# The feed-forward up-projection's low parts leave GpSimd, its product moves ahead of the next convolution, and the routing's long steps take one operand from PSUM

## The reference, cut to what matters

```python
v1, i1 = lax.top_k(sc[..., 0, :], 16)
v2, i2 = lax.top_k(sc[..., 1, :], 16)
cand = (v1[..., :, None] + v2[..., None, :]).reshape(B, S, 8, 256)
cidx = (i1[..., :, None] * 128 + i2[..., None, :]).reshape(B, S, 8, 256)
best, pos = lax.top_k(cand, 16)
idx = jnp.take_along_axis(cidx, pos, axis=-1)
```

```python
up = hn @ w_up                                   # 1024 -> 2 x 2816
gate = gelu(causal_dwconv(up[..., :2816], conv_f_w, conv_f_b))   # 3 taps along the tokens
return (gate * up[..., 2816:]) @ w_down
```

## Time and profile before

| | us |
|---|---|
| median of 3 runs (lowest, highest) | 1558.96 (1558.39, 1559.15) |
| the profiled execution, its own time | 1558.32 |
| its span in the profile | 1556.3 |
| TensorE busy (PE) | 1465.7 (94%) |
| VectorE busy (DVE) | 1059.1 (68%) |
| ScalarE busy (ACT) | 719.7 (46%) |
| GpSimd busy (POOL) | 326.4 (21%) |
| mean DMA rate | 157 GB/s |

### The profile page before, as it was taken

How to read it: one execution, slowest core, us unless ns; L and a number is a source line. 1 busy time by engine, 2 the same in 40 slices (tenths; PEclk the granted TensorE clock), 3 DMA queues, 4 the chain that set the end, 5 groups by cost and what they waited for, 6 DMA issues and landing times.

```text
span 1556.3 us, 26173 instructions
## 1 busy us (share of the span) xinstructions
PE 1465.7 (94%) x10784; PEld 1323.0 (85%) x10784; DVE 1059.1 (68%) x1702; ACT 719.7 (46%) x1031; POOL 326.4 (21%) x158
## 2 busy tenths in 40 slices
PE   7989989999999999999999999999986889988998
PEld 7989879989999999998887888887974678888876
DVE  5565664886937777788888756555797844577764
ACT  5762554544444344444444455445541544544443
POOL 4000000698980000000000000001252420233310
PEclk9999999999999999999999999999997999999999
DMA  6334455455555555455554575554421343444553
GB/s 230 125 122 136 125 180 192 133 168 181 171 174 171 164 163 162 157 165 165 165 163 163 190 244 191 189 189 150 136 95 54 109 149 109 151 158 152 163 181 116
DMA packets 66933, 245.11 MB, mean 157 GB/s; under 512 B 7424, under 2 KB 7552, under 8 KB 66560
## 3 DMA queue, kind: packets, MB, share of 16 engines
q1 hardware_dynamic: 66816, 243.45, 47.9%
HBM read 242.37 MB, written 1.05 MB: 156 GB/s over the span
## 4 chain that ended last, share of the span: by engine, by line
PE 73%; DVE 13%; ACT 7%; POOL 4%; issue 2%; DMA 0%; DVEq 0%; ACTq 0%; POOLq 0%
PE bank L415 73%; DVE A L1474 4%; DVE A L1467 4%; ACT whi L999 4%; POOL wlo L2236 3%; ACT A L999 2%; DVE A L1471 2%; DVE wlo L1471 1%; PE bank L424 1%; DVE A L1468 1%; ACT L999 1%; DVE A L2013 0%; POOL small L2242 0%; DMA xres<-in_x 0%; DVE hTl L1474 0%
## 5 line engine op out<-in xcount | busy, mean ns | idle before, releaser
L999 ACT ACTIVATE whi<-raw 128x1024 fp32r<-128x1024 f32 x448 | 471.9, 1056 | 423.0 <-PE bank L415 422.0
L1471 DVE TENSOR_TENSOR wlo<-raw,whi 128x1024 fp32r<-128x1024 f32 x333 | 408.1, 1228 | 318.7 <-ACT whi L999 318.3
L415 PE MATMUL bank<-hTh,whi 128*128 128x256 f32 x1944 | 560.5, 288 | 28.0 <-DVE wlo L1471 15.1
L415 PE MATMUL bank<-hTh,wlo 128*128 128x256 f32 x1944 | 550.3, 283 | 0.0
L415 PE MATMUL bank<-hTl,whi 128*128 128x256 f32 x1944 | 549.5, 283 | 0.0
L415 PEld LDWEIGHTS bank<-hTh,whi 128*128 128x128 f32 x1944 | 368.1, 189 | 37.8 <-DVE wlo L1471 19.2
L2236 POOL TENSOR_TENSOR wlo<-raw,whi 128x1024 fp32r<-128x1024 f32 x115 | 298.1, 2601 | 410.0 <-ACT whi L999 406.4
L415 PEld LDWEIGHTS bank<-hTl,whi 128*128 128x128 f32 x1944 | 369.2, 190 | 0.8 <-issue 0.7
L415 PEld LDWEIGHTS bank<-hTh,wlo 128*128 128x128 f32 x1944 | 367.7, 189 | 0.0
L415 PE MATMUL bank<-whi,hTh 128*128 128x512 f32 (+2 forms) x552 | 217.9, 395 | 4.2 <-POOL wlo L2236 2.3
L415 PE MATMUL bank<-wlo,hTh 128*128 128x512 f32 (+2 forms) x552 | 215.0, 390 | 0.0
(11 more groups left out here) (151 smaller groups left out, 1487.4 us busy)
## 6 DMA issues: line engine op xcount, KB each, us to landing
raw<-in_u SPq DMA_DIRECT2D x128, 512.0 KB, 3.3
raw<-in_v SPq DMA_DIRECT2D x128, 512.0 KB, 3.4
raw<-in_w_up SPq DMA_DIRECT2D x44, 512.0 KB, 3.3
raw<-in_w_down SPq DMA_DIRECT2D x22, 512.0 KB, 4.1
raw<-in_w_in_t SPq DMA_DIRECT2D x18, 512.0 KB, 3.7
raw<-in_w_in_g SPq DMA_DIRECT2D x16, 512.0 KB, 3.4
raw<-in_w_out SPq DMA_DIRECT2D x16, 512.0 KB, 3.4
raw<-in_w_pq SPq DMA_DIRECT2D x16, 512.0 KB, 4.3
```

The lines of the kernel that those rows point to most:

```text
L415: return e.matmul(o, l, r, start=st, stop=sp_, skip_group_check=True)
L999: return e.activation(o, i, func, **kw)
L1471: return e.tensor_tensor(o, a, b, op)
```

## The change

It has three parts.

1. `on_pool` no longer gives GpSimd the odd units that are prepared during the up-projection: 22 low parts move to VectorE (units 3 to 43 of `w_up` and unit 1 of `w_down`). Unit 1 of `w_up` stays on GpSimd.
2. In VectorE's `lin_T`, `after(u)` becomes `before(u)`: the product of pair j-1 is issued ahead of the wait for pair j and of its convolution.
3. In the routing, `iota16` and a copy of the second half of the values are put into PSUM bank 7; the one-hot comparison reads `iota16` there and writes to banks 0 to 3 in four pieces of 512; the product reads those banks, in four pieces; the sum for `cand` reads the copy in bank 7.

```diff
 def on_pool(i):
     slot = i - 2
     if BASE["u"] <= slot < BASE["u"] + 62:
         return True
-    if BASE["w_up"] <= slot < BASE["w_up"] + 44:
-        return i % 2 == 1
     if slot == BASE["w_xk"] or i in (1, BASE["w_pq"] + 1, BASE["w_up"] + 1):
         return True
...
-            def lin_T(u0, units, evict=None, after=None, per=1, steps=(1,)):
+            def lin_T(u0, units, evict=None, before=None, per=1, steps=(1,)):
                 for u in range(units):
                     i = u0 + u
                     lo(i + 2)
+                    if before:
+                        before(u)
                     if (u + 1) * per % 2 == 0:
                         q = pair[0]
                         if evict:
                             e.wait_ge(s["w"], i + 1)
                             evict((u + 1) * per - 2, t3(banks[4 + q % 3][:, :], 2))
                         pair[0] += 1
-                    if after:
-                        after(u)
                     side.step(steps[(i + 1) % len(steps)])
...
                 shape = [P, 8, 16, 16]
+                v2p = t3(banks[7][:, 16:16 + P], 8)
+                own(e.tensor_copy(v2p, vv[:, :, 1, :]))
                 again()
                 own(tt(t4(cand, 8, 16), vv[:, :, 0, :].unsqueeze(3).to_broadcast(shape),
-                       vv[:, :, 1, :].unsqueeze(2).to_broadcast(shape), ALU.add))
+                       v2p.unsqueeze(2).to_broadcast(shape), ALU.add))
...
                 for q in range(2):
                     ps = t3(posf[:, q * P:(q + 1) * P], 8)
-                    o4 = t4(oh, 8, 16)
+                    part = [P, 2, 16, 16]
                     again()
-                    own(tt(o4, ps.unsqueeze(3).to_broadcast(shape),
-                           K_("iota16").unsqueeze(1).unsqueeze(1).to_broadcast(shape), ALU.is_equal))
+                    for g in range(4):
+                        own(tt(t4(banks[g][:, :], 2, 16), ps[:, 2 * g:2 * g + 2, :].unsqueeze(3).to_broadcast(part),
+                               banks[7][:, 0:16].unsqueeze(1).unsqueeze(1).to_broadcast(part), ALU.is_equal))
                     again()
-                    own(tt(t4(oh2, 8, 16), o4, iv[:, :, q, :].unsqueeze(2).to_broadcast(shape), ALU.mult))
+                    for g in range(4):
+                        own(tt(t4(oh2[:, g * 512:(g + 1) * 512], 2, 16), t4(banks[g][:, :], 2, 16),
+                               iv[:, 2 * g:2 * g + 2, q, :].unsqueeze(2).to_broadcast(part), ALU.mult))
...
+            own(e.tensor_copy(banks[7][:, 0:16], K_("iota16")))
             own(e.tensor_copy(t3(iota_b[:, :], P), K_("iota").unsqueeze(2).to_broadcast([P, P, 2])))
             lin_T(BASE["w_pq"], 16)
```

More of the change, by code:

```diff
@@ L327, in build @@
         candw = a2(24064, 2048)
-        oh = a2(26112, 2048)
         oh2 = a2(28160, 2048)
```

## The result

| | before | after | ratio (95%) |
|---|---|---|---|
| median, us | 1558.68 (4 runs) | 1533.37 (4 runs) | 0.9838 (0.9808 to 0.9868) |
| lowest to highest | 1557.89 to 1559.15 | 1529.98 to 1536.88 | |
| profiled execution, us | 1558.32 | 1530.26 | |
| its span | 1556.3 | 1528.0 | |

The change is faster by 1.6%. The forecast was 1530.1 us, in a range of 1528.0 to 1540.5. The profiled execution is the one to compare with the forecast's sum (1529.5), since both are one execution; it took 0.8 us more.

What follows compares the result with a forecast made beforehand. It took the up-projection to be bound by a ring of waits and the routing by GpSimd's low parts. 18.8 + 1.1 + 8.9 = 28.8 us off 1558.32 gave 1529.5, forecast as a median of 1530.1, range 1528.0 to 1540.5.

Steps and rivals of the forecast that it cites:

- The hold: Up-projection: GpSimd's low part holds VectorE's tensor_scalar, which opens a convolution, at 2.29 us; without it 0.35.
- The up-projection, 18.8 us: Parts one and two bring 145.55 us down to 126.7, 22 pairs at 5.76 us; bounds 18.8 and 9.4.
- The ring: Up-projection waits before the change: gate copy, convolution, product, R4h, high part, Gelu, next high part, next gate copy; 6.71 us a turn.
- the new ring: Up-projection after the change: convolution, Gelu, high part, low part, product; 4.52 us, 5.0 with hand-overs, against 5.76 allowed.
- w_down, 1.1 us: Third unit of w_down: its 0.91 us wait for a low part goes, 1.1 us with the restart.
- The routing, 8.9 us: TensorE's losses to GpSimd's slowed low parts, 4.8 and 4.1 us in two blocks, are gained; GpSimd at 2.43 us.
- Pieces at 0.68 us: Routing: a VectorE piece of 512 with a PSUM input takes 0.68 us, sixteen of them 10.9 us a block.
- The cover: Routing, second block: VectorE idles 12.58 us for TensorE's pass 30, so the block may grow by 12.6 us without cost.
- The copy into bank 7: Routing: by the skill's rule VectorE's copy of values into PSUM may be held by GpSimd; at most 2.4 us, covered.
- the routing gave its gain: Answers the rival that the routing gives nothing and its 8.9 us stay: 1539.0 us, chance 0.10.
- the stage kept nothing of its loss: Answers the rival that the up-projection keeps half, TensorE waiting some 0.4 us a pair: 1539.5 us, chance 0.10.
- the tensor_scalar went to 0.35 us: Answers the slower rival: the tensor_scalar stays at 2.29 us, held by something other than GpSimd; 1566.4 us, chance 0.03.

Runs made afterwards that it cites:

- the all-SBUF pieces: The kernel after with the routing's pieces of 512 kept but every operand, including the cand sum's, in SBUF: 1550.69 us, routing stretch 464.0 us.
- the kernel with half the steps in PSUM: The kernel after with the one-hot comparison writing to SBUF, so the products read two SBUF inputs in pieces of 512: 1531.59 us, routing stretch 448.3.

## Why the prediction was right, point by point

- *The hold.* "GpSimd's step holds it, and its length is not its own": right, shown twice over by the 0.35 us of the tensor_scalar without GpSimd and by the hold that moves to the tap once the tensor_scalar has a PSUM operand.
- *The up-projection, 18.8 us.* Measured 18.6, at 126.9 us. The reason was half right. The ring and its slow link were as read, and TensorE waits for nothing in the stage now. But the prediction said that parts one and two "must be taken together", and each alone gives all of it: part one with a ring of 5.76 us, just at the bound, part two with 2.53 us of slack in front of the convolution. The way of counting the new ring (4.52 us, 5.0 with hand-overs), whole durations and hand-overs end to end, comes out too long, since an instruction begins before its forerunner's printed end (without the reordering VectorE's low part at 1404.55 lasts 1.22 us, and the next step starts at 1405.68). Here it erred to the safe side; without the reordering it made me expect 134 us or more.
- *w_down, 1.1 us.* Measured 1.2 at the third unit, whose wait is gone, and 1.2 to the end.
- *The routing, 8.9 us.* Measured 9.0; GpSimd at 2.4 us a part and no wait of TensorE for it. Counting by pace and not by the 6.9 us of printed waits was right: the run without part three has 7.0 us of waits and 9.0 us more time. That the cure is the PSUM operand and not the cutting is shown by the all-SBUF pieces.
- *Pieces at 0.68 us.* 0.69, writing to PSUM included, and started every 0.60 us. The cover in the second block was 16.63 us, more than the 12.58 counted on.
- *The copy into bank 7.* The prediction allowed, from the Trainium skill's rule, that it "may be held". It was not: in both blocks it begins 0.01 or 0.02 us behind the start of a low part of GpSimd and takes 0.28 us.
- *Not in the sum.* The head of the kernel, which the change barely touches (one copy of 0.17 us), came out 1.0 us shorter and the stretch of the second layer 1.5 us longer. The head is chance: the kernel with half the steps in PSUM has 226.3 us there again. In the second layer the granted clock is 0.95 and 0.88 from 1070 to 1090 us, where the kernel before has 1.00 over the same work. The two nearly cancel, and that they do is luck.
- *The median.* The sum was good to 0.5 us (28.3 of span against 28.8). The median was 3.3 us above the forecast, since "a microsecond or two either way" was too little. TensorE's half clock in the first layer (last section) costs 6 us where it shows; that it is what lifted the median is likely but not shown, since the two longer runs were not profiled.
- *The rivals.* None came: the routing gave its gain, the stage kept nothing of its loss, the tensor_scalar went to 0.35 us.

## What to carry to other kernels

Where a short VectorE step looks long, set its end against GpSimd's ends: if the two go together, the step is being held, its busy time is not work, and an engine that seems full may have room. Give such a step a PSUM operand or shift it in time, but look which instruction stands next with its tensors in SBUF, since the hold can go there; and don't cut an SBUF step into pieces beside an engine that is always ready to start. A ring of waits costs only what it exceeds the bound by, so of two cures that shorten it one may do; check how much slack that one leaves. Add up a ring from starts, not from printed durations.

## What the runs showed of the hardware that I had not expected

**A cut makes the loser.** Beside back-to-back low parts of GpSimd, an SBUF step of 2048 elements takes 4.36 us and slows GpSimd to 3.40 us a part on average; four steps of 512 take 11.19 us and GpSimd 2.82 us a part. Nothing but the length of the pieces was changed in the product step.

**Half clock without a pause, in some executions.** Of the fourteen executions whose profiles are kept, six have a stretch of low clock in the first layer, between 150 and 168 us, and reach the start of the routing stretch 5 to 8 us later than the eight others, which have 1.00 there: 231.3 to 232.9 us against 225.2 to 226.3. Which edit the kernel had makes no difference. The windows of one of the six, the kernel without the reordering (PEclk is the third number from the end):

```profile
148.00:152.00 4.00, 4.00 (x39) 4.00 (x37) 0.75 (x2) 0.00 (x0) 0.00 (x0) 1.00 0.37 131
152.00:156.00 4.00, 4.00 (x25) 4.00 (x24) 0.42 (x1) 0.00 (x0) 0.00 (x0) 0.59 0.00 0
156.00:160.00 4.00, 4.00 (x20) 4.00 (x21) 0.42 (x1) 0.00 (x0) 0.00 (x0) 0.50 0.02 4
160.00:164.00 4.00, 4.00 (x20) 4.00 (x20) 1.03 (x2) 2.00 (x2) 0.00 (x0) 0.50 0.00 0
164.00:168.00 4.00, 4.00 (x27) 4.00 (x26) 0.86 (x2) 1.80 (x3) 0.00 (x0) 0.70 0.40 131
```

and of one of the eight, the repeat of the kernel after, over the same work:

```profile
156.00:160.00 4.00, 4.00 (x35) 4.00 (x35) 1.46 (x2) 3.24 (x4) 0.00 (x0) 1.00 0.00 0
```

TensorE runs at 0.50, the lower of the two levels (1.2 GHz), for some 13 us, having been busy without a pause in the window before and during it; the first matmul of the next step starts at 173.6 us, and in the repeat at 166.0. Why it happens in one execution and not in the next, no run here tells.
